# Late modulation chunks: weight blocks summed on VectorE beside the gate and branch products, TensorE summing over partitions once per chunk

## What is computed

```
mod_ctx = jax.nn.silu(c_ctx) @ w_mod[l] + b_mod[l]          # context tokens
mod_lat = (jax.nn.silu(c) @ w_mod[l] + b_mod[l])[:, None, :] # latent tokens
shift, scale, gate = jnp.split(mod, 3, axis=-1)              # 3 x 1024 columns
u = (layer_norm(x) * (1.0 + scale) + shift)
...
merged = sum(gb * ((yb * jax.nn.silu(zb)) @ w_branch[i]) for i, (yb, zb, gb) in ...)
h = alpha * x + gate * (merged @ w_out)
x_new = (layer_norm(h) * ln_g + ln_b)
```

## Time and profile before

| | |
|---|---|
| runs | 1556.05, 1557.13, 1558.44 us |
| median | 1557.13 us |
| span of the profiled execution, first to last instruction | 1555.3 us |
| median less span | 1.8 us |
| PE busy | 1519.7 us, 98% of the span |
| DVE, ACT, POOL busy | 743.9, 473.8, 629.2 us |
| granted PE clock, mean | 0.998 |

### The profile page before, as it was taken

How to read it: one execution, slowest core, us unless ns; L and a number is a source line. 1 busy time by engine, 2 the same in 40 slices (tenths; PEclk the granted TensorE clock), 3 DMA queues, 4 the chain that set the end, 5 groups by cost and what they waited for, 6 DMA issues and landing times.

```text
span 1555.3 us, 22672 instructions
## 1 busy us (share of the span) xinstructions
PE 1519.7 (98%) x9091; PEld 1248.3 (80%) x9091; DVE 743.9 (48%) x1467; ACT 473.8 (30%) x1099; POOL 629.2 (40%) x501
## 2 busy tenths in 40 slices
PE   8999999999999999999999999999999999999997
PEld 6798788885788887788878977889768888778886
DVE  5596710646423333622497584125680136262257
ACT  1246710155410123411144485012671003232010
POOL 3551045600145453145773401555104554423562
PEclk9999999999999999999999999999999999999999
DMA  9420022317222222025431100222311221211421
GB/s 339 114 72 29 1 68 68 108 60 244 69 68 82 68 68 61 28 77 180 121 127 42 58 15 14 68 82 82 100 41 55 81 82 55 68 49 44 173 81 68
DMA packets 80488, 128.72 MB, mean 83 GB/s; under 512 B 16444, under 2 KB 29184, under 8 KB 80384
## 3 DMA queue, kind: packets, MB, share of 16 engines
q1 hardware_dynamic: 78144, 122.03, 24.8%
q10 hardware_dynamic: 2240, 5.24, 0.9%
HBM read 120.96 MB, written 6.30 MB: 82 GB/s over the span
## 4 chain that ended last, share of the span: by engine, by line
PE 82%; DVE 8%; POOL 3%; ACT 2%; issue 2%; DMA 2%; SPq 0%; POOLq 0%; DVEq 0%; ACTq 0%
PE pb L1018 55%; PE pb L1163 5%; PE pb L1292 4%; PE pb L1043 3%; PE pb L1243 3%; PE pb L1206 2%; PE pb L962 1%; PE pb L1214 1%; PE pb L1473 1%; DMA raw<-in_w_mod 1%; PE pb L1336 1%; DVE ks L2138 1%; DMA raw<-in_w_in 1%; POOL slot_T L857 1%; ACT pr L1749 1%
## 5 line engine op out<-in xcount | busy, mean ns | idle before, releaser
L1018 PE MATMUL pb<-wsp,act_T 128*128 128x512 f32 x3048 | 713.5, 392 | 4.4 <-DVE act_T L2077 2.0
L1018 PEld LDWEIGHTS pb<-wsp,act_T 128*128 128x128 f32 x3048 | 568.3, 188 | 128.8 <-issue 7.1
L854 POOL CAST wsp<-raw 128x1024 fp32r<-128x1024 f32 x128 | 136.5, 1067 | 804.3 <-PE pb L1018 651.6
L857 POOL TENSOR_TENSOR wsp<-raw,wsp 128x512 fp32r<-128x512 f32 x268 | 360.2, 1365 | 10.2
L1018 PE MATMUL pb<-wsp,yT 128*128 128x512 f32 x720 | 165.7, 390 | 0.0
L1018 PEld LDWEIGHTS pb<-wsp,yT 128*128 128x128 f32 x720 | 135.1, 188 | 27.9
L2610 DVE SCALAR_TENSOR_TENSOR mt<-tg,pb 128x512 f32<-128x512 f32 x40 | 27.4, 686 | 216.6 <-PE pb L1018 215.8
L1903 ACT ACTIVATE tg<-pb 128x512 f32<-128x512 f32 x60 | 35.9, 599 | 275.9 <-PE pb L1018 275.9
L1749 ACT ACTIVATE pr<-pb,nm 128x640 f32<-128x640 f32 (+2 forms) x128 | 91.4, 714 | 2.5 <-DVE nm L2279 2.4
L1243 PE MATMUL pb<-ident,pr 128*128 128x128 f32 x480 | 73.7, 274 | 2.6 <-ACT pT L1784 2.3
L2309 DVE TENSOR_SCALAR pr<-pr,rden 128x640 f32<-128x640 f32 (+2 forms) x128 | 70.9, 554 | 4.5
(11 more groups left out here) (301 smaller groups left out, 1963.1 us busy)
## 6 DMA issues: line engine op xcount, KB each, us to landing
raw<-in_w_in SPq DMA_DIRECT2D x112, 512.0 KB, 3.4
raw<-in_w_mod SPq DMA_DIRECT2D x32, 512.0 KB, 4.3
raw<-in_w_branch SPq DMA_DIRECT2D x24, 512.0 KB, 3.6
raw<-in_w_out SPq DMA_DIRECT2D x16, 512.0 KB, 3.7
stage<-in_w_mod SPq DMA_DIRECT2D x28, 256.0 KB, 7.2
raw<-in_w_in SPq DMA_DIRECT2D x16, 256.0 KB, 5.4
xh<-in_x_sample SPq DMA_DIRECT2D x6, 512.0 KB, 5.9
out<-xh ACTq DMA_DIRECT2D x5, 512.0 KB, 2.9
```

The costliest lines, as they stand in the source:

```text
L854: pool.tensor_copy(hi, raw[:, p % 3, :, 0:width]).then_inc(raw_hi, 1)
L857: ins = pool.tensor_tensor(lo[:, j, :], raw[:, p % 3, j, 0:width], hi[:, j, :].bitcast(F32), ALU.subtract)
L1018: mm = pe.matmul(dst, lhs(a, k, t), w[:, wa, j, 0:width], start=(k == 0 and n == 0), stop=(i == count - 1 and j == 1 and n == 2))
```

## The change

The eight late chunks leave C's loop, and most of their arithmetic leaves PE. DVE now goes through the eight blocks (k) of a chunk and, for each of the two rows (w), multiplies the 128 x 512 block by the row's value in each partition and adds it up in `mod_sum`: 16 steps to a chunk, the first two plain multiplications (TENSOR_SCALAR), the other 14 SCALAR_TENSOR_TENSOR with two inputs in SBUF. What is left is the sum over the partitions, which PE does once per chunk with a column of ones for each row (`pick_row`): 8 matmuls in place of 32. The steps lie beside A's products in layer 0 (chunks 0 to 3), C's in layer 0 (4, 5) and A's in layer 1 (6, 7). The blocks get six buffers of their own, over the queries and keys of the attention that has ended, and SP loads them behind a wait for that attention's context scores. `gates` moves from C's first G to the start of B, and the order in which PSUM banks come round shifts.

```diff
-LATE_CHUNKS = (((1, 0), (1, 2), (1, 1), (1, 3), (0, 4), (0, 5)), ((1, 4), (1, 5)))
-MOD_AT = ((*range(2, 8), *range(10, 28)), (2, 4, 6, 8, 10, 12, 14, 16))
+LATE_CHUNKS = [(1, 0), (1, 2), (1, 1), (1, 3), (0, 4), (0, 5), (1, 4), (1, 5)]
+MOD_SLOTS = 6
+MOD_STEPS = 16
+LATE_AT = {(0, "A"): (0, 4), (0, "C"): (4, 6), (1, "A"): (6, 8)}
+LATE_LOADS = {(0, "A"): {2: range(0, 6), 6: (6,), 7: (7,), 8: (8, 9), 9: (10,), 10: (11, 12), 11: (13, 14), 12: (15,)},
+              (0, "C"): {2: range(16, 22), 6: (22,), 8: (23,)}, (1, "A"): {2: range(24, 30), 6: (30,), 8: (31,)}}
+LATE_SUMS = {(0, "A", "BR", 0, 0, 4): ("sum", 0), (0, "A", "BR", 0, 1, 2): ("turn", 0),
+             (0, "A", "G", 1, 0, 4): ("sum", 1), (0, "A", "G", 1, 1, 4): ("turn", 1),
+             (0, "A", "G", 1, 3, 2): ("sum", 2), (0, "A", "BR", 1, 0, 4): ("turn", 2),
+             (0, "C", "q", 0, 1, 4): ("sum", 3), (0, "C", "q", 0, 2, 4): ("turn", 3),
...
 # SP
+                def load_late(m):
+                    ll, c = LATE_CHUNKS[m // 4]
+                    if m >= MOD_SLOTS:
+                        sp.wait_ge(mod_used, m - MOD_SLOTS + 1)
...
+                    for br in ("A", "C"):
+                        n = p - pieces.first[l, (br, "G", 0)]
+                        for m in LATE_LOADS.get((l, br), {}).get(n, ()):
+                            if n == 2:
+                                wait_full(sp, (br, "Sctx"))
+                            load_late(m)
 # PE
+                def late_sum(n):
+                    key, (ll, c) = ("gmod", n), LATE_CHUNKS[n]
+                    acquire(key)
+                    pe.wait_ge(pick_zero, 2)
+                    pe.wait_ge(mod_used, 4 * (n + 1))
+                    b = bank_of(key)
+                    for w in range(2):
+                        for q in range(4):
+                            pe.matmul(pb[32 * q:32 * q + 32, b, 0:P], pick_row[:, w, :], mod_sum[:, n % 2, w, tile_cols(q)],
+                                      start=(w == 0), stop=False)
+                    modulation_bias(b, ll, range(4 * c, 4 * c + 4)).then_inc(*full(key))
...
-                        if br == "C":
-                            late_step(s)
...
                     if br == "B":
+                        gates()
                         mlstm()
 # DVE
+                def late(br, count):
+                    first, last = LATE_AT.get((l, br), (0, 0))
+                    for n in range(late_next[0], min(late_next[0] + count, MOD_STEPS * (last - first))):
+                        chunk, k, w = first + n // MOD_STEPS, n % MOD_STEPS // 2, n % 2
+                        m = 4 * chunk + k // 2
+                        to, src = mod_sum[:, chunk % 2, w, :], mod_raw[:, m % MOD_SLOTS, k % 2, :]
+                        by = csil[:, k, w:w + 1]
...
+                        if k == 0:
+                            ins = dve.tensor_scalar(to, src, by, None, ALU.mult)
+                        else:
+                            ins = dve.scalar_tensor_tensor(out=to, in0=src, scalar=by, in1=to, op0=ALU.mult, op1=ALU.add)
...
+                    late(br, 12)
                     gate_context()
                     y_lo_context()
+                    late(br, 8 if (l, br) == (0, "A") else 4)
...
+                        if (l, br) in LATE_AT:
+                            if (l, br) == (0, "A"):
+                                if hf == 0:
+                                    late_row(0)
+                                else:
+                                    late(br, 10)
+                                    late_row(1)
+                                    late(br, 8)
+                                    late_columns(1)
+                                    late(br, 4)
+                                    late_row(2)
+                            else:
+                                if hf:
+                                    late(br, 16)
+                                late_row(LATE_AT[l, br][0] + hf)
                         for t in range(T):
...
+                            if (l, br) == (0, "A"):
+                                if (hf, t) == (1, 0):
+                                    late_columns(2)
+                                late(br, 2)
+                                if (hf, t) == (0, T - 1):
+                                    late_columns(0)
+                                elif (hf, t) == (1, T - 1):
+                                    late(br, 4)
```

More of the change, by code:

```diff
@@ L231, with late_banks @@
 O_BANKS = ((5, 5, 5, 5), (5, 6, 5, 2))
[L234 to L242, removed]
+def late_banks(psum, *place):
+    if place in LATE_SUMS:
+        what, n = LATE_SUMS[place]
+        if what == "sum":
+            psum.roll(("gmod", n))
+        else:
+            psum.roll(("gmodT", n))
 def plan_layer(l, pieces, psum):
@@ L290, in plan_layer @@
                         psum.roll((br, name, t))
+                    for n, t in ((n, t) for n in range(4) for t in range(T)):
+                        late_banks(psum, l, br, name, 0, n, t)
                     continue
@@ L329, in plan_layer @@
         else:
+            for i in range(4):
+                psum.roll(("gate", i))
             for name, col in (("qk", 0), ("gates", None), ("v", 512), ("T", None), ("o", 1024)):
@@ L368, in plan_layer @@
                     psum.roll((br, name, hf, t))
+                for n, t in ((n, t) for n in range(4) for t in range(T)):
+                    late_banks(psum, l, br, name, hf, n, t)
                 if br != "B" and (name, hf) == ("G", 0):
@@ L372, in plan_layer @@
                         psum.roll(key)
-                    if br == "C":
-                        for i in range(4):
-                            psum.take(("gate", i), psum.use[l, keys[i % 3]][0])
                 if (br, name, hf) == ("B", "G", 0):
@@ L518, in trunk_kernel @@
         kT = at("kT", [P, KV, 2, TOK + P], F32R, arena + 67072)
+        mod_raw = at("mod_raw", [P, MOD_SLOTS, 2, HALF], F32, arena + 46592)
+        mod_sum = at("mod_sum", [P, 2, 2, HALF], F32, arena + 71168)
         tg = at("tg", [P, T, HALF], F32, arena + 23040)
@@ L1108, in gates, with late @@
                         mm.then_inc(*full(("gate", i)))
[L1110 to L1129 removed]
+                def late_sum(n):
[9 more added lines that the diff above has]
+                    modulation_bias(b, ll, range(4 * c, 4 * c + 4)).then_inc(*full(key))
+                def late(*place):
+                    if place in LATE_SUMS:
+                        what, n = LATE_SUMS[place]
+                        if what == "sum":
+                            late_sum(n)
+                        else:
+                            wait_done(pe, ("gmod", n))
+                            turn_chunk(("gmodT", n), n)
                 def attention(br):
@@ L1134, in attention @@
                     if br == "C":
-                        project((br, "q"))
+                        project((br, "q"), after=lambda i, t: late(l, br, "q", 0, i, t))
                     def turned(what, t):
@@ L1318, in context @@
                             values_context()
-                        if br == "C" and (i, t) == (2, T - 1):
-                            gates()
                     return context
@@ L1810, in attention @@
                         .then_inc(y_hi[l], 1)
-                    if br == "C":
-                        act.wait_ge(stored[l], 64)
-                        for i in range(4):
-                            wait_full(act, ("gate", i))
-                            act.copy(gate_bc[:, i // 2, (i % 2) * HALF:(i % 2 + 1) * HALF], bank(("gate", i)))\
-                                .then_inc(*done(("gate", i)))
-                def mlstm():
+                def mlstm():
+                    act.wait_ge(stored[l], 64)
+                    for i in range(4):
+                        wait_full(act, ("gate", i))
+                        act.copy(gate_bc[:, i // 2, (i % 2) * HALF:(i % 2 + 1) * HALF], bank(("gate", i)))\
+                            .then_inc(*done(("gate", i)))
                     for t in range(T):
@@ L1980, in _ @@
             dve.memset(ones[:, :], 1.0).then_inc(first_stat, 1)
+            dve.memset(pick_row[:, :, :].rearrange("p w k -> p (w k)"), 0.0).then_inc(pick_zero, 1)
+            dve.wait_ge(pick_zero, 1)
+            for w in range(2):
+                ins = dve.memset(pick_row[:, w, w:w + 1], 1.0)
+            ins.then_inc(pick_zero, 1)
             def first_stats(t):
```

105 lines of the change are left out of this document (50 added, 55 removed), and 2 rows, old and new, of the table LATE_SUMS.

## The result

The changed kernel takes 1562.01 us (median of 9 runs, 1561.29 to 1563.98), the kernel before in the same series 1558.44 (9 runs). The ratio is 1.0027, 95% interval 1.0017 to 1.0036: slower by 0.27%, where 0.44% faster was forecast, and outside the range of 1544 to 1559 us. The profiled execution has a span of 1560.5 us, 5.2 more than that of before, and a mean granted clock of 0.995. The two medians are only 3.6 us apart: the profiled execution of before took 1.3 us less than the median of its nine runs, that of after 0.5 us more than its own. What follows explains the 5.2 us of the spans.

The account below looks back on a forecast made before the run. PE, busy 1519.7 of 1555.3 us, was taken to bound the kernel. -20.9 + 7.4 + 0.4 + 0.7 + 5.5 = -6.9 us gave a span of 1548.4, 1550.2 us with 1.8 between span and median; range 1544 to 1559 us.

Parts of the forecast that it names:

- DVE's delay, 5.5 us forecast: A's products, layer 0: PE waits for DVE's sums at two narrow places, 1.8 and 3.7 us, together 5.5 us.
- the first narrow place: A's layer 0, first half from its first BR tile: DVE's 32nd step ends 14.1 us in, PE waits 1.8 us.
- The walk for the second: Second half's narrow place: some 5.3 us of DVE waits, steps taking 15.9 us, PE waiting 3.7 us.
- DVE's delay into C's keys is taken up by C's query product of four pieces.: Layer 0, from A into C: DVE's lateness for C's keys was taken to cost PE nothing.
- rival (2): DVE late by 11.3 us in A's products: 1556.0 us, or 1561.4 if PE's clock falls twice; chance 0.2, 0.12 with clock.
- the three signs of being wrong: `mod_sum` waits over 9 us in sum, granted clock under 1.00 inside A's products, or C's loop over 57 us.
- They alternate, one of each every 1.66 us: A's products: DVE's steps and POOL's split passes on SBUF inputs take turns, one of each every 1.66 us.
- C's loop, -20.9 forecast: C's loops without the chunks shrink to 55.2 us: layer 0 by 16.8 us, layer 1 by 4.1, together 20.9.
- Rival (3): C's loop shrinks less, its round of scores, exponential and transposes setting it: 1551.4 us at worst; chance 0.53 together with the forecast.
- layer 1 holds this twice: Layer 1's C loop: four bursts and a bias are worth 2.04 us, twice, so 4.1 us come off, leaving 55.2.
- A sum, 0.92 us forecast: PE's sum per chunk among the products: 8 matmuls 0.57 plus bias 0.35, 0.92 us, eight times 7.4 us.
- `wcb`, 0.7 us forecast: Layer 0's B: `wcb` gets the bank of the last o tile, so PE waits 0.7 us for ACT's tanh.

Follow-up runs that it names:

- thin steps: The changed kernel with each of DVE's 112 multiply-and-add steps on 32 of its 512 columns, the rest left out of the sums: 1550.66 us, 0.9956.
- bursts_later: The kernel before, with layer 1's eight bursts in steps 10 to 24 of C's loop instead of 2 to 16: 1558.54 us, 1.0006.
- mended_held: Changed kernel: chunk 3's row earlier, two banks rechosen, sums 1 and 2 later, second split at C's loop start held until step 31: 1546.26 us, 0.9928.
- pairs: The changed kernel, with sums 4 and 5 side by side in C's second BR half, 6 and 7 likewise in layer 1's A: 1561.56 us, 1.0027.

## Why the prediction was wrong

**DVE's delay, 5.5 us forecast, 10.0 measured.** The walk for the first narrow place was right: it put the 32nd step 14.1 us behind the first BR tile and PE's wait at 1.8; 14.0 and 1.86 were measured. The walk for the second gave 15.9 us for DVE's steps, and they took 17.3 (275.32 to 292.6), near its upper bound. The step that failed stands behind it: "DVE's delay into C's keys is taken up by C's query product of four pieces." I had put the sum of chunk 3 behind the first piece of that product, 12.2 us behind the first tile, and priced a wait of 3.7 us there. It stands behind the second, 18.9 us behind the tile, and doesn't wait; but its transpose is due 8.0 us after it, and DVE's row stands in DVE's order behind the whole key path. I never walked DVE's queue from its last step to that copy. With a start of the key path 12.2 us into the product (1.4 before), and remainders that alternate with POOL's passes (10.8 us to their end, 5.6 before), it was late by 4.54 us. Moving the copy took all of it away.

The clock's 2.6 us were priced in rival (2), at 2.7, and this rival came true in part: the time lies just above its upper value (1562.0 against 1561.4), but by one long wait instead of two, and with 7.0 us of waits for DVE and for the POOL that it held (1.86, 0.61 and 4.54), not 11.3. Of the three signs of being wrong only one showed, a loop of C over 57 us: the waits for `mod_sum` came to 1.9 us and not to 9, and in A's products the clock was kept. No sign pointed at `mrow`.

**POOL as the one that is held.** "They alternate, one of each every 1.66 us" holds for POOL's TENSOR_TENSORs. A CAST beside steps that follow each other without a gap took 4.24 us and 3.85 (at 251.33 and 197.19), about four times its 1.04. That brought the wait of 0.61 us for `wsp`. With thin steps no CAST takes more than 1.50 and this wait is gone.

**C's loop, -20.9 forecast, -17.9 measured, and +1.3.** Rival (3) came true, by another mechanism than it named. The round of the loop didn't set a floor: the third eight steps took their 12.65 us. The chunks' blocks had kept `raw` full, so that POOL's first split of C's G pieces began 9.6 us into layer 0's loop and 10.2 us into layer 1's (before):

```profile
344.97 1.04 POOL L854 CAST wsp<-raw 128x1024 fp32r<-128x1024 f32 x1 [37.11 <-DMA raw<-in_w_in]
...
1112.16 1.04 POOL L854 CAST wsp<-raw 128x1024 fp32r<-128x1024 f32 x1 [37.40 <-DMA raw<-in_w_in]
```

Without them the second one runs beside the loop's first units and costs 1.1 us in each layer. Of the 3.0 us missing this is 2.2, shown by holding it back. The other 0.8 are in the reading "layer 1 holds this twice". It took the second and the third eight steps for equally long when bare, and the first four bursts for as dear as the second four. Bare, the second eight take 11.92 us and the third 12.65, so four bursts and a bias were worth 14.68 - 11.92 = 2.8 us there (2.3 in `bursts_later`), not 2.04, but at the loop's start 0.9 at most: 3.7 us in sum instead of 4.1 (59.33 less the 55.67 of the bare loop, which `mended_held` has in both layers), and so 0.4 us less gain than forecast. Layer 0 was counted down to the same bare loop and misses the same 0.4. Those 3.7 us hold what the splits inside the loop cost before; how much of them are the bursts' own stays open. The wait for `prc` is a second bank of the shifted ring. I looked for such waits in layer 0's B and wrote that the ring costs one.

**A sum, 0.92 us forecast, 1.165 measured**, eight times: 1.9 us. I had added the lengths of its two groups and left out what the interrupted products lose, 0.25 us.

**`wcb`, 0.7 us forecast.** The wait was 0.78, at the forecast place. Unforeseen were the 1.6 us of low clock behind it.

Right were the gates (nothing, from the start of C's first G half to B, without the first BR half, 33.11 + 40.80 us before against 29.49 + 45.46 with one sum), the transposes, the dates of the loads (neither PE nor DVE waits for a late block), and that layer 1 has no wait for `mod_sum`. A slip in the chances: by their own rule those for faster by over 0.2% add up to 0.75, not 0.73. All errors but the last are of one sign: +4.5 for DVE and clock, +3.0 and +1.3 for the loops, +1.9 for the sums, +1.7 at `wcb`, +0.1 for the transposes, less 0.4 of drift. Together 12.1 us, the distance from -6.9 to +5.2.

## What to carry to other kernels

When work moves to a helper engine, walk that engine's queue from the moved work to every later point where the bound engine waits for it, also in the next stage; the price was not beside the moved steps but 14 us behind them, at a small copy placed behind strangers. Removing transfers lets others come earlier: ask which engine starts sooner then, and beside what. A change that is right in its parts can lose by a few placements; a ledger of stage distances finds them. The row and the banks, mended alone, gave what their forecasts said (6.9 and 3.8 us by the medians). The later sums gave more than their forecast (2.9 us in A's products where 1.9 were expected, and 0.8 of clock). The splits gave their 2.2 us only at the second place tried for them; at the first the kernel lost 4 us.

## What the runs showed of the hardware

PE's clock can fall behind waits much shorter than the 4.54 us, and shorter than the 3 us from which rival (2) counted it. Behind the 0.78 us wait for `zo` and the narrow transposes that follow, the granted clock was 0.50 for about 3 us in five of six traces that have this wait, and in none of the seven without it; behind the 1.86 us wait for `mod_sum` it fell in one trace of five (`pairs`, the next 30 matmuls 8.72 us instead of 7.12). What decides in a single execution stays open: no run here separates it.

The DVE and GpSimd conflict is not symmetric in its price. DVE's steps in a row (eight in 6.16 us, 0.77 us each, against six in 4.05, 0.67 each, with POOL idle) held one CAST for 4.24 us and slowed little themselves; the short DVE operations of the loop were the ones held, 0.92 us for 0.16.
